# Half products from two units earlier, with eight modulation operations behind each ordinary unit

## What is computed

```python
def swiglu(h, wi, wo):
    gu = h @ wi
    return (jax.nn.silu(gu[..., :D_FF]) * gu[..., D_FF:]) @ wo

def trunk_layer(x, mod, lw, ctx, pos):
    ...
    h = rmsnorm(x, ng[0]) * (1.0 + m(1)) + m(0)
    x = x + 0.5 * m(2) * rmsnorm(swiglu(h, lw['ffn_wi'][0], lw['ffn_wo'][0]), ng[1])
    ...
```

## Time and profile before

| | |
|---|---|
| time, median of 3 executions | 3053.07 us (3049.8 to 3058.28) |
| the profiled execution's own time | 3051.59 us |
| its span, first to last instruction | 3049.8 us |
| TensorE busy (PE), matmuls | 2910.4 us, 26152 |
| VectorE busy (DVE) | 2166.0 us |
| ScalarE busy (ACT) | 1294.8 us |
| matmuls of ordinary units (L2606), one of three operand pairs | 406.8 us, 1632 |
| matmuls of half products (L2672) | h pairs 3 x 864, sum pairs 3 x 648 |
| chain that ended last, by engine | PE 80%, DVE 10%, ACT 3%, issue 3%, DMA 3% |

### The profile page before, as it was taken

How to read it: one execution, slowest core, us unless ns; L and a number is a source line. 1 busy time by engine, 2 the same in 40 slices (tenths; PEclk the granted TensorE clock), 3 DMA queues, 4 the chain that set the end, 5 groups by cost and what they waited for, 6 DMA issues and landing times.

```text
span 3049.8 us, 62386 instructions
## 1 busy us (share of the span) xinstructions
PE 2910.4 (95%) x26152; PEld 2601.7 (85%) x26152; DVE 2166.0 (71%) x3223; ACT 1294.8 (42%) x2165; POOL 416.7 (14%) x465
## 2 busy tenths in 40 slices
PE   6999999999988899999999999999998889999998
PEld 5999878996777689998799998799876777999986
DVE  4987586756666788876878776767566767787635
ACT  3135454235533451454532554532454435345434
POOL 1000111002333220001100001110033333100100
PEclk8999999999989999999999999999998999999999
DMA  6522444410000244225452225453010004312234
GB/s 250 201 70 84 152 153 152 179 46 27 30 4 14 99 173 166 70 70 187 145 193 90 90 70 200 145 177 130 15 52 8 3 13 161 111 70 84 83 124 172
DMA packets 92915, 325.10 MB, mean 107 GB/s; under 512 B 10288, under 2 KB 13936, under 8 KB 77296
## 3 DMA queue, kind: packets, MB, share of 16 engines
q1 hardware_dynamic: 92656, 321.39, 29.7%
HBM read 318.05 MB, written 3.31 MB: 105 GB/s over the span
## 4 chain that ended last, share of the span: by engine, by line
PE 80%; DVE 10%; ACT 3%; issue 3%; DMA 3%; POOL 0%; SPq 0%; ACTq 0%; DVEq 0%; POOLq 0%
PE PS L2606 22%; PE PS L2672 20%; PE PS L2719 18%; PE PS L2616 3%; PE PS L812 2%; DMA wo<-in_wo 2%; PE PS L1584 2%; PE PS L836 1%; PE PS L1563 1%; DVE wo_lo L3131 1%; ACT wo_hi L2838 1%; PE PS L759 1%; PE PS L1576 1%; DMA wm<-in_wm 1%; PE PS L824 1%
## 5 line engine op out<-in xcount | busy, mean ns | idle before, releaser
L2606 PE MATMUL PS<-h_hi,wi_hi 128*128 128x384 f32 (+2 forms) x1632 | 406.8, 311 | 11.2 <-issue 11.2
L2719 PE MATMUL PS<-wo_hi,a_hi 128*128 128x512 f32 x968 | 391.6, 405 | 19.3 <-DVE wo_lo L3131 12.7
L2606 PE MATMUL PS<-h_hi,wi_lo 128*128 128x384 f32 (+2 forms) x1632 | 403.8, 309 | 0.0
L2606 PE MATMUL PS<-h_lo,wi_hi 128*128 128x384 f32 (+2 forms) x1632 | 403.7, 309 | 0.0
L3131 DVE TENSOR_TENSOR wo_lo<-wo,wo_hi 128x1024 fp32r<-128x1024 f32 x208 | 255.4, 1228 | 193.2 <-ACT wo_hi L2838 192.6
L2719 PE MATMUL PS<-wo_hi,a_lo 128*128 128x512 f32 x968 | 378.6, 391 | 0.0
L2719 PE MATMUL PS<-wo_lo,a_hi 128*128 128x512 f32 x968 | 378.0, 390 | 0.0
L2838 ACT ACTIVATE wo_hi<-wo 128x1024 fp32r<-128x1024 f32 x208 | 220.2, 1059 | 304.8 <-PE PS L2719 206.6
L3191 DVE TENSOR_TENSOR part_lo<-wi,part_hi 128x512 fp32r<-128x512 f32 x378 | 255.5, 689 | 105.2 <-ACT part_hi L2872 102.2
L2872 ACT ACTIVATE part_hi<-wi 128x512 fp32r<-128x512 f32 x378 | 236.1, 630 | 190.5 <-PE PS L2672 118.8
L2606 PEld LDWEIGHTS PS<-h_hi,wi_hi 128*128 128x128 f32 (+1 forms) x1632 | 262.4, 188 | 15.4 <-issue 13.4
(11 more groups left out here) (370 smaller groups left out, 5813.2 us busy)
## 6 DMA issues: line engine op xcount, KB each, us to landing
wi<-in_wi SPq DMA_DIRECT2D x88, 1024.0 KB, 4.8
wo<-in_wo SPq DMA_DIRECT2D x176, 512.0 KB, 3.2
wm_in<-in_wm SPq DMA_DIRECT2D x104, 512.0 KB, 3.7
wi<-in_win SPq DMA_DIRECT2D x24, 1024.0 KB, 5.2
wo<-in_wout SPq DMA_DIRECT2D x32, 512.0 KB, 3.2
wm_out<-in_wm SPq DMA_DIRECT2D x24, 512.0 KB, 4.4
wm<-in_wm SPq DMA_DIRECT2D x4, 2048.0 KB, 17.7
wq<-in_wq SPq DMA_DIRECT2D x2, 1024.0 KB, 4.7
```

Source lines behind the costliest of these rows:

```text
L2606: mm = pe.matmul(PSF[0:cols, at:at + GW[g]], st, h[:, k, GA[g]:GA[g] + GW[g]], start=(k == 0 and q == 0), stop=(k == KD - 1 and q == 2))
L2719: mm = pe.matmul(PS[:, OUT_BANK[t] + half, :], a, w[:, (V0(n) + b) % 2, kk, :], start=(u == 0 and kk == 0 and q == 0), stop=True, skip_gro ...
```

## The change

Two constants. In all four feed-forward sub-layers the half products begin two units sooner (eight units in all are converted), and eight modulation operations instead of seven stand behind each ordinary unit.

```diff
@@ -54,7 +54,7 @@
-FFN_AHEAD, FFN_MOD = 8, 7
+FFN_AHEAD, FFN_MOD = 8, 8
@@ -123,7 +123,7 @@
-FAST = {0: 10, 2: 10, 3: 8, 5: 6}
+FAST = {0: 8, 2: 8, 3: 6, 5: 4}
```

## The result

The changed kernel takes 3095.86 us, the median of 4 runs (3091.0 to 3101.73), against 3055.68 (3049.8 to 3058.44) of the kernel before: a ratio of 1.0133 [1.0116, 1.015], or +40.2 us between the medians. The forecast was 3092.1 us, from a sum of +40.5.

The account below looks back on a forecast made before the run. TensorE bounds the kernel on average, but DVE is already the late engine at the switch. Half-product units add 98.6 us, earlier sums take off 58.1: +40.5 on 3051.6 gives 3092.1 us, range 3080 to 3106.

Parts of the forecast that it names:

- sums start after t0: DVE's sums of h start 87.4, 87.4, 58.3, 29.1 us after a sub-layer's first modulation operation, if DVE never waits.
- two more half-product units, four times: Two more half-product units (24.64 us) follow the sums in each of four sub-layers: 98.6 us in all.
- The rigid stretch: From the start of the sums to the seventh product, taken as unchanged 36.7 us in all four sub-layers.
- the first two shadows of the third: Stalls before unit 3 and the last ordinary unit only change where TensorE idles, not when the sums end.
- in front of the partition matmuls: TensorE's wait for the last fold before the last ordinary unit: 4.3 us in sub-layers 0 and 2, 3.4 and about 2.5 in 3 and 5.
- In front of the first product: TensorE idle 6.6 us between the last ordinary unit and the first half product, where the kernel before had none.
- The wait of unit 3 for its cut: TensorE waits about 0.7 us before unit 3, because a fold stands ahead of its weight cut.
- almost wholly behind DVE: At the switch, 6 us of slow TensorE clock stay hidden: cost taken as 0, up to 3 us per switch without slack.
- The rival that priced it at 12 us: Clock falls and recovers late: 3 us or a little more per switch, +12 or so, 3104 us; chance 0.12.
- One check of the list: Among the signs to look for in the changed profile: TensorE busy some 14 us less.
- Stays hidden: Modulation work stays hidden under the ordinary units, so the change gains 14.1 us: 3037.5 us; chance 0.03.
- Only the last batch is late: DVE catches up before the last batch, so each switch shifts by that batch's operations alone: +18, 3070 us; chance 0.06.

Follow-up runs that it names:

- eight operations alone: Kernel before with eight instead of seven modulation operations behind each unit, half products where they were: 3058.14 us against 3056.09, ratio 1.0005.
- earlier in sub-layer 0 only: Changed kernel with the half products' earlier start kept in sub-layer 0 and put back in the three others: 3069.02 us against 3056.09 of the kernel before, ratio 1.004.
- narrowed, before: Kernel before with feed-forward modulation accumulations, except each row's first, cut from 1024 to 128 columns: 3053.70 us against 3056.09, ratio 0.9991.
- narrowed, changed: Changed kernel with feed-forward modulation accumulations, except each row's first, cut to 128 columns, folds full width: 3065.12 us, ratio 1.0032 to the kernel before.
- narrowed, changed, folds earlier: Changed kernel with accumulations cut to 128 columns and ten instead of eight modulation operations behind each unit: 3046.81 us against 3055.63 of the kernel before, ratio 0.9968.
- three more additions: Kernel before with three extra 128 x 1280 DVE additions at the head of the sums of h: 3078.39 us against 3055.63, ratio 1.0077.
- nine-step sums, before: Kernel before with the sums of h formed in nine additions instead of ten, using a third buffer: 3054.26 us, ratio 0.9995.
- nine-step sums, changed: Changed kernel with the sums of h formed in nine additions instead of ten, using a third buffer: 3100.36 us, ratio 1.0145 to the kernel before.
- partition matmuls moved: Changed kernel with the partition matmuls moved from ahead of the last ordinary unit into its middle: 3095.39 us against 3055.43 of the kernel before, ratio 1.0137.
- and the fold moved: Changed kernel with partition matmuls inside the last ordinary unit and the fold put behind unit 3's weight cut: 3096.22 us, ratio 1.0141 to the kernel before.
- sums on GpSimd: Changed kernel with the ten additions of the sums of h moved from DVE to GpSimd during ordinary units, four buffers: 3165.21 us, ratio 1.0362 to the kernel before.
- and both moves: Changed kernel with the sums of h on GpSimd, plus the moved partition matmuls and moved fold: 3142.18 us, ratio 1.029 to the kernel before.

## Why the prediction was right

**The sum.** Its terms, against distances within the profiled execution (us; earlier start of the sums in sub-layers 0, 2, 3, 5):

| term | predicted | measured |
|---|---|---|
| sums start after t0 | 87.4, 87.4, 58.3, 29.1 | 87.41, 87.41, 58.17, 28.93 |
| earlier than before by | 13.8, 13.8, 14.7, 15.8 | 13.77, 13.76, 14.84, 15.94 (58.3 in all) |
| sums to seventh product | 36.7 | 36.69, 36.67, 36.64 (sub-layers 2, 3, 5) |
| two more half-product units, four times | 98.6 | 99.2 (25.2, 24.6, 24.6, 24.7) |
| whole change | +40.5 | +40.8 by distances, +40.2 by the medians |

The distance for the whole change runs from t0 to ACT's last copy of a half product (`f_p`) in the same sub-layer. In sub-layer 2 it is 1379.67 - 1113.09 = 266.58 us before and 1405.32 - 1127.87 = 277.45 after, +10.9:

```profile
1379.67 0.44 ACT L2901 ACTIVATE f_p<-PS 128x320 f32<-128x320 f32 x1 [1.32 <-PE PS L2672]
```

```profile
1405.32 0.44 ACT L2901 ACTIVATE f_p<-PS 128x320 f32<-128x320 f32 x1 [1.32 <-PE PS L2672]
```

The four sub-layers give 11.5 + 10.9 + 9.8 + 8.7 = +40.8. The same sum for the other runs, against the kernel before, leaves out the mixers and their scatter (us):

| kernel | by distances | by medians |
|---|---|---|
| eight operations alone | +3.7 | +2.1 |
| earlier in sub-layer 0 only | +14.2 | +12.9 |
| narrowed, before | -0.1 | -2.4 |
| narrowed, changed | +8.8 | +9.0 |
| narrowed, changed, folds earlier | -9.8 | -8.8 |
| three more additions | +21.1 | +22.8 |
| nine-step sums, before | -0.5 | -1.4 |
| nine-step sums, changed | +39.6 | +44.7 |
| partition matmuls moved | +40.8 | +40.0 |
| and the fold moved | +41.1 | +40.8 |
| sums on GpSimd | +110.3 | +109.8 |
| and both moves | +84.4 | +86.8 |

But for one row (nine-step sums, changed, 5.1 apart) the two columns agree to 2.5 us, which is what the medians can tell: what every one of these edits costs lies between t0 and the end of the half products. That the medians came within 0.3 us of the forecast is finer than they can measure; that the distances did is not luck, since each term holds by itself.

The first line of the first table was the risk, and it held to 0.2 us because DVE never waited in the shortened loop; a plain sum of instruction prices was enough. The rigid stretch was a choice, and three more additions, each paid in full, show that it was the right one.

**The stalls.** Their order and places were right, and so was calling the first two shadows of the third, which the moved partition matmuls and the moved fold show. Sizes: in front of the partition matmuls 4.3 in sub-layer 0, 3.3 in 3 and 3.1 in 5 (predicted 4.3, 3.4, 2.5). In front of the first product 4.0 to 6.4 instead of 6.6: in sub-layer 2 the last ordinary unit ended 17.1 us after the sums, where the prediction had 14.4, because it ran in part at half clock behind its own pause (next paragraph). The product itself came when predicted, 21.1 us after the sums. The wait of unit 3 for its cut is there too, 1.9 us in 3 waits of up to 0.6.

**The clock.** The pauses did bring the clock down. Stretches of the changed kernel in sub-layers 0 and 2 (us; busy PE, PEld, DVE, ACT, POOL; PEclk, DMA share, GB/s), to be read beside the earlier trace rows:

```profile
171.60:176.00 4.40, 0.64 (x4) 0.65 (x5) 4.37 (x9) 0.00 (x0) 0.00 (x0) 1.00 0.01 2
176.00:182.00 6.00, 4.67 (x22) 4.41 (x20) 5.17 (x9) 4.54 (x8) 0.00 (x0) 0.72 0.00 0
182.00:190.00 8.00, 7.03 (x37) 7.06 (x38) 7.13 (x12) 3.83 (x9) 0.00 (x0) 0.79 0.39 133
1236.00:1242.00 6.00, 5.62 (x23) 5.63 (x24) 5.14 (x9) 3.51 (x6) 0.00 (x0) 0.55 0.00 0
1242.00:1252.00 10.00, 7.94 (x52) 7.24 (x50) 9.13 (x16) 5.49 (x13) 0.00 (x0) 1.00 0.29 106
```

Behind the idle of 3.99 in sub-layer 2 the granted clock was 0.55 for 6 us, mostly the 1.2 GHz level, and back at 1.00 before the third product, which starts 28.7 us after the sums in both kernels, with or without the dip: DVE's work sets it. In sub-layer 0 it was below full twice (0.72, then 0.79) and cost 0.6 us: the same copy in the next unit comes 41.1 us after the sums there, against 40.5 in sub-layer 2. That was predicted as "almost wholly behind DVE". The rival that priced it at 12 us had the mechanism and not the price. What the prediction overlooked is a second dip: it looked at the pause in front of the first product only, and the one in front of the partition matmuls lowered the clock too, in three sub-layers (0.63 from 151 to 157 in 0, 0.51 from 1214 to 1221 in 2, 0.78 from 2686 to 2692 in 5; 1.00 from 1651 to 1657 in 3). It cost no time, because the last ordinary unit had 6.6 us to spare.

**One check of the list missed.** TensorE's busy time should have fallen by 14 us; it rose by 12.4 (2910.4 to 2922.8), though there is less work. The mean granted clock went from 0.981 to 0.971, and the mean of a matmul from 311 to 315 ns at L2606 (the ordinary units, and the mixers' products of the same form, which the table of the profile before counts with them) and from 309 to 312 in half products. At L2719, whose products stand away from the switch, it stayed at 405. Busy microseconds count a slow matmul longer, so they are no measure of work where the clock moves; the count of matmuls is. This line carried nothing in the sum.

**The rivals.** "Stays hidden" needed the sums 28.2 us earlier; they came 14 to 16 earlier, and the narrowed kernel with early folds shows that 3 of 4 sub-layers reach its condition once DVE's load is gone, with 9.7 us of its gain of 14.1. "Only the last batch is late" was given 3070 for the changed kernel and became true of the narrowed one, at 3065.12: the last batch alone already costs more than the eight converted units bring.

**What stays open.** Of the runs that keep the whole arithmetic none beat the kernel before by more than a measurement can tell. Moving the modulation work elsewhere instead of leaving it out, a nine-step sum with ACT's rounding in time, and the folds alone put earlier at full width were not tried. That GpSimd's additions are what slows DVE rests on their coming at one pace and ending together; no run put them at another place.

## What to carry to other kernels

Before moving a boundary, count what the in-order engine beside it must finish ahead of it, instruction by instruction from one row each, and ask when it gets there if it never waits. The same modulation work was hidden behind eight ordinary units and was not behind six: a shorter cover costs what it no longer covers, whatever the busy shares of the whole kernel say. To test for slack, add a known piece of work to the suspected stretch and see whether it is paid in full.

## What was unexpected of the hardware

- GpSimd and DVE slowed each other on SBUF operands: float32 accumulations of 128 x 1024 on DVE went from 1.2 to 3.85 us each while GpSimd added tiles of 128 x 1280, a cut of 128 x 2048 from 2.28 to 4.17, and GpSimd's own additions took 2.95 for the first and 3.74 for most of the others. An operation of DVE with an input in PSUM kept its 0.87.
- Behind the four pauses of 4.0 to 6.4 us in front of the first half product, TensorE ran in part at its lower clock (a granted clock of 0.55 to 0.79 over the next 6 to 8 us), at the cost of 0.6 us in one sub-layer and of nothing in the others, because DVE was later still.
- The same dip can cost more where DVE is less late. Three additions of 4.57 us at each switch cost 18.3 us, and the copies behind the first half-product unit come 21.1 us later in all: 1.6 us more than the additions in sub-layer 0, 0 in 2, and 0.6 in 3 and 5. In sub-layer 0 the granted clock was 0.59 from 200.7 to 206.7 and TensorE busy all of that time, so nothing hid it. The interval by the medians is 19 to 28 us.
